# Adding two channel chunks on GpSimd ahead of a LayerNorm mean, in a two-layer hybrid decoder trunk

## What is computed

```python
def conformer_conv_mixer(z, w_conv, b_conv, ln_g, ln_b):
    a, g = jnp.split(z, 2, axis=-1)
    u = a * jax.nn.sigmoid(g)
    u = causal_dwconv(u, w_conv) + b_conv.astype(u.dtype)     # 31 taps
    return jax.nn.silu(layernorm(u, ln_g, ln_b))
```

## Time and profile before

| | before |
|---|---|
| median of 3 runs (lowest to highest) | 1189.68 us (1189.12 to 1189.72) |
| the profiled execution | 1188.96 us |
| span from its first to its last instruction | 1187.0 us |
| outside the span | 1.96 us |
| TensorE busy | 98% of the span |
| VectorE busy | 68% |
| ScalarE busy | 49% |
| GpSimd busy | 18% |

### The profile page before, as it was taken

How to read it: one execution, slowest core, us unless ns; L and a number is a source line. 1 busy time by engine, 2 the same in 40 slices (tenths; PEclk the granted TensorE clock), 3 DMA queues, 4 the chain that set the end, 5 groups by cost and what they waited for, 6 DMA issues and landing times.

```text
span 1187.0 us, 15228 instructions
## 1 busy us (share of the span) xinstructions
PE 1165.6 (98%) x5938; PEld 987.3 (83%) x5938; DVE 812.5 (68%) x1081; ACT 580.9 (49%) x879; POOL 213.7 (18%) x201
## 2 busy tenths in 40 slices
PE   7999989999999999999999999999999999999998
PEld 6897878898888888888898887888888888888886
DVE  5799786786666666544759887858766666664464
ACT  4455585644444444434444647855444444443432
POOL 2375372100000000000016834712000000000000
PEclk9999999999999999999999999999999999999999
DMA  8233343533333333566633333345333323236564
GB/s 255 79 88 86 93 134 99 164 94 106 106 90 96 100 96 100 176 190 216 194 100 87 89 91 80 107 142 160 91 105 92 104 89 107 89 102 200 176 225 148
DMA packets 155178, 146.81 MB, mean 124 GB/s; under 512 B 4800, under 2 KB 135780, under 8 KB 155108
## 3 DMA queue, kind: packets, MB, share of 16 engines
q1 hardware_dynamic: 154528, 145.12, 40.6%
q10 hardware_dynamic: 579, 0.74, 0.2%
HBM read 139.54 MB, written 2.10 MB: 119 GB/s over the span
## 4 chain that ended last, share of the span: by engine, by line
PE 91%; DVE 4%; ACT 2%; issue 1%; POOL 1%; DMA 0%; DVEq 0%; POOLq 0%; ACTq 0%
PE ps L578 29%; PE ps L579 29%; PE ps L580 29%; PE ps L914 1%; PE ps L640 1%; PE ps L889 1%; DVE negmax L1358 1%; POOL cf_out L1016 1%; DVE hid L1374 1%; PE ps L860 1%; ACT prob L1692 1%; DMA x<-in_x 0%; PE ps L723 0%; DVE xn L1138 0%; PE ps L716 0%
## 5 line engine op out<-in xcount | busy, mean ns | idle before, releaser
L578 PE MATMUL ps<-xn,wsp 128*128 128x512 f32 (+1 forms) x1120 | 412.1, 368 | 0.7
L580 PE MATMUL ps<-xn,wsp 128*128 128x512 f32 (+1 forms) x1120 | 409.1, 365 | 0.0
L579 PE MATMUL ps<-xn,wsp 128*128 128x512 f32 (+1 forms) x1120 | 408.9, 365 | 0.0
L473 DVE TENSOR_TENSOR wsp<-raw,wsp 128x1024 fp32r<-128x1024 f32 (+2 forms) x249 | 307.0, 1236 | 148.3 <-ACT wsp L465 147.9
L465 ACT ACTIVATE wsp<-raw 128x1024 fp32r<-128x1024 f32 (+2 forms) x256 | 266.3, 1041 | 166.4 <-PE ps L580 124.0
L578 PEld LDWEIGHTS ps<-xn,wsp 128*128 128x128 f32 x1120 | 211.4, 189 | 36.6 <-DVE xn L1138 2.1
L579 PEld LDWEIGHTS ps<-xn,wsp 128*128 128x128 f32 x1120 | 211.4, 189 | 33.7 <-issue 0.5
L580 PEld LDWEIGHTS ps<-xn,wsp 128*128 128x128 f32 x1120 | 211.3, 189 | 33.5
L578 PE MATMUL ps<-wsp,hid 128*128 128x512 f32 (+1 forms) x488 | 190.3, 390 | 0.0
L580 PE MATMUL ps<-wsp,hid 128*128 128x512 f32 (+1 forms) x488 | 189.3, 388 | 0.0
L579 PE MATMUL ps<-wsp,hid 128*128 128x512 f32 (+1 forms) x488 | 189.2, 388 | 0.0
(11 more groups left out here) (163 smaller groups left out, 1190.8 us busy)
## 6 DMA issues: line engine op xcount, KB each, us to landing
raw<-in_w_ffn_up SPq DMA_DIRECT2D x88, 512.0 KB, 3.8
raw<-in_w_ffn_down SPq DMA_DIRECT2D x88, 512.0 KB, 3.9
raw<-in_w_in SPq DMA_DIRECT2D x36, 512.0 KB, 3.9
raw<-in_w_out SPq DMA_DIRECT2D x32, 512.0 KB, 3.8
x<-in_x SPq DMA_DIRECT2D x4, 512.0 KB, 8.1
xn<-xn SPq DMA_DIRECT2D x8, 256.0 KB, 3.2
raw<-in_w_vkr SPq DMA_DIRECT2D x4, 432.0 KB, 3.3
out_x<-x SPq DMA_DIRECT2D x3, 512.0 KB, 5.3
```

The costliest lines, as they stand in the source:

```text
L473: eng.tensor_tensor(wsp[:, u % SPLIT, 1, 0:nk * n], raw[:, (l * NU + u) % RAW, 0:nk * n], fp(wsp[:, u % SPLIT, 0, 0:nk * n]), ALU.subtract ...
L578: pe.matmul(dst, a[0], b[0], start=start, stop=False, skip_group_check=True)
L579: pe.matmul(dst, a[0], b[1], start=False, stop=False, skip_group_check=True)
L580: return pe.matmul(dst, a[1], b[0], start=False, stop=stop, skip_group_check=True)
```

## The change

GpSimd adds the two chunks into `cf_tmp[:, 0, :]`, behind `rsqrt("ckv")` and ahead of `sums("cq")`, waiting for `cf_conv` and for its own last `cf_sum`; it raises a new semaphore `cf_both`. TensorE waits for `cf_both` and does one product with the matrix of ones.

```diff
         cf_norm = sem("cf_norm")
+        cf_both = sem("cf_both")
         cf_affine = sem("cf_affine")
...
                             dense(g, bank_of(g), x_pairs, ks=range(1, 4))
-                            pe.wait_ge(cf_conv, l + 1)
-                            pe.wait_ge(cf_sum, (l + 1) * (CF_TAPS - 1))
-                            for c in range(2):
-                                last = pe.matmul(ps[:, CF_BANK, :], ones[:, :], cf_out[:, c, :], start=c == 0, stop=c == 1)
-                            last.then_inc(mean_done, 1)
+                            pe.wait_ge(cf_both, l + 1)
+                            pe.matmul(ps[:, CF_BANK, :], ones[:, :], cf_tmp[:, 0, :], start=True, stop=True)\
+                              .then_inc(mean_done, 1)
                             last = dense(g, bank_of(g), x_pairs, ks=range(4, KD))
...
                 rsqrt("ckv", l)
+                pool.wait_ge(cf_conv, l + 1)
+                pool.wait_ge(cf_sum, (l + 1) * (CF_TAPS - 1))
+                pool.tensor_tensor(cf_tmp[:, 0, :], cf_out[:, 0, :], cf_out[:, 1, :], ALU.add).then_inc(cf_both, 1)
                 sums("cq", l)
                 sums("ln", l)
```

## The result

The changed kernel takes 1191.74 us (median of 11 executions, 1190.93 to 1194.48), the kernel before 1189.52 us (11 executions): ratio 1.0023, interval 1.0014 to 1.0032. By the medians it is slower by 2.2 us; forecast were +2.6 us and 1192.3 us. The ratio is that of the means, 1192.25 and 1189.50 us, which lie 2.75 us apart.

The account below looks back on a forecast made before the run. TensorE, busy 98%, was taken as the bound; VectorE's lateness of 1.37 us would make it 1.29 us late, over two layers 2.6: 1188.96 becomes 1191.5, plus 0.72 for the median, 1192.3 us. Range 1190.9 to 1193.3.

Parts of the forecast that it names:

- Part 2: New add on GpSimd, held by VectorE's line 473: TensorE waits 0.67 us at the mean, keeping 0.19 of 0.86.
- Part 3: VectorE's queue behind the add: cq sums and VectorE's instructions take turns, making VectorE 1.37 us late.
- the second rival: GpSimd keeps SBUF for its next instruction or gets it first: VectorE 1.66 us late, +3.2 us, 1192.8; chance 0.20.
- The third: Rival: VectorE's tensor_scalar, line 1299, isn't held by GpSimd: VectorE 1.1 us late, +2.0 us, 1191.7; chance 0.21.
- The first rival: GpSimd finds its turns free, so VectorE isn't late: -0.2 us, 1189.5; chance 0.09.
- part 1: At the mean, TensorE loses one fp32 product: 0.86 us per layer off its stream.
- the slack of 0.08 us: At stat("ln") in layer 0, the ln sum is ready 0.08 us before TensorE comes.
- s: VectorE's lateness at the end of its queue (line 1227), forecast 1.37 us; TensorE leaves late by s - 0.08.
- Nothing on a clock of its own: Behind this stage everything follows TensorE, so its delay of 1.29 us in layer 0 stays to the end.

Follow-up runs that it names:

- e1: Kernel before plus the new add on GpSimd, its sum unused; TensorE keeps both products and its waits, VectorE waits for the add: 1191.74 us against 1189.75.
- e2: Kernel before with one product and no add on GpSimd, chunk 0 left out of the mean: 1188.98 us against 1189.75.
- e7: Kernel before with one product (chunk 0 left out), no add, and stat and spread of cq and ln later on TensorE: 1188.67 us against 1189.34.
- e10: As e7, but with both spreads earlier, directly behind the first k-step of group 19: 1187.51 us against 1189.51.
- e8: Changed kernel with four more matmuls ahead of stat("cq"), in TensorE's pause: 1191.24 us against 1189.75 for the kernel before.
- e6: Kernel before, both products kept, with stat and spread of cq and ln later in TensorE's stream: 1190.60 us against 1189.34.

## Why the prediction was right

The direction, the mechanism and its places were as forecast; that the median came as close to 1192.3 us as it did is in part luck (below). The places, step by step (layer 0, minus the 0.59 us that the whole stage lay later in the profile after):
- **Part 2**: the add was held behind the first line 474 and ended 1.14 us behind it (forecast 1.15). TensorE waited for it: about 0.7 us (0.67).
- **Part 3**: the two engines alternated. The first cq sum ended 1.15 us behind the second line 474, the second 1.15 behind the first line 1304 (703.60 + 1.48 = 705.08 for 703.18 + 0.75 = 703.93 in layer 1). So the second rival, GpSimd keeping SBUF for its next instruction, fell. The third fell too: the tensor_scalar was held, 0.80 us for 0.49. On the Trainium skill's rule on it ("SBUF — State Buffer", section "Who interferes with whom") the trace agrees that it takes turns; whether by the mode that the page names, no run here shows.
- **The first rival**, free turns, is excluded by e1: the add by itself costs 2.0 us, at a full clock and with no wait at the mean.
- **The gain of part 1** was worth no more than the slack of 0.08 us here; e2 shows it alone, and e7 and e10 show it whole once the meeting is elsewhere.

Two sizes were off. **The terms of part 3** were too large: I took a held instruction to be 0.13 us shorter than its own length behind the add that held it. That is so for line 474. The tensor_scalar ended 0.28 us behind the sum (115.91 for 115.63), where 0.36 was forecast, and the second line 1304 0.56 behind (118.41 for 117.85), where 0.62 was. From the spread of ckv to the end of line 1229 VectorE needs 120.14 - 109.91 = 10.23 us for 118.33 - 109.32 = 9.01: s = 1.22 us, not 1.37, and TensorE is late by 1.12 per layer and not by 1.29. Two layers give 2.2 us. From 100 us to the end of the span, by the start times of the same weight loads, after loses 2.1 us when the clock's 1.19 and the transfer's 0.8 are taken off, e1 2.0 (less 0.3 for the same transfer) and e8 2.0. The medians show a little less: +1.6 us for the seven executions at a full clock (median 1191.10), +2.0 for e1, +1.5 for e8.

**The clock was left out.** I read the granted clock of before and gave the new pauses no effect on it. Four of 11 executions have a lower clock and lie 2.6 us above the others. In the one of them that was traced 1.2 us are the clock's and 0.8 the late transfer's, and 0.6 lay ahead of the stage; how the other three divide is not known. They make the spread (3.5 us from lowest to highest, 1.0 before) and lift the median from 1191.10 to 1191.74, and that is the luck: terms of part 3 that were too large and a clock term that was missing cancel in part. At a full clock the forecast of +2.6 us was 1.0 us too high by the medians, 0.4 by the traces of the stage.

**"Nothing on a clock of its own"** behind the stage was too simple. A transfer of `ml_rope` whose time to land varied from 2.7 to 4.4 us held TensorE in attention in the profile after, and a delay of VectorE reaches TensorE there over GpSimd (e6).

Left open: why that transfer lands late in some traces, and how much of the spread of every kernel's times it makes.

## What to carry to other kernels

Work moved to GpSimd is not free because GpSimd is idle: look at what VectorE runs at that minute, and put GpSimd's instructions where VectorE reads PSUM; the same three adds cost 1.2 us of VectorE in one order and 0.3 in another. Work taken off the busiest engine counts only up to its next meeting with a slower queue, so read the slack at each such meeting first, and move the meeting together with the saving, with a run that moves it alone as a control: here the first new place cost 1.2 us by itself. A new pause of more than a microsecond on TensorE should be filled, or its price reckoned with what the clock may do behind it.

## What the runs showed that I had not expected

- With a pause of 1.3 us in each layer, on a TensorE that is otherwise busy 98% of the time, 4 of 11 executions had a lower clock; the traced one had 3.4 us at half clock behind one of its two pauses (granted 0.50, matmuls every 0.43 us for 0.23). With 2.7 us of pause it was 5 of 5, in the traced one for 6.8 us. Four matmuls worth nothing, put into the pause, took the effect away.
- A VectorE instruction held by GpSimd ends sooner behind it than its own length: by 0.13 us for line 474 (1.09 for 1.22) and for line 1199 in the earlier trace rows (0.55 for 0.68), by 0.2 us for the tensor_scalar (0.28 for 0.49) and for line 1304 (0.56 for 0.75).
- The later spreads of e6, with no wait added on TensorE, cost 1.2 us: an engine with 98% of busy time had a second queue behind it, over VectorE and GpSimd to attention, that was no looser than a microsecond.
